# Retention phase: the order of score masks, convolution norm and gates on three engines

## The chip, the core and the metric

The kernel runs on one core of a Trainium2 chip. The metric is the device time of one execution in microseconds. The core's engines run side by side, each through its own instruction queue in order: TensorE (PE, matrix products into PSUM), VectorE (DVE), ScalarE (ACT), GpSimd (POOL) and SyncE (SP, which here only issues DMAs). They are coordinated by semaphores that the program writes out by hand.

## The reference, cut to what is touched

One encoder layer in fp32: 2048 tokens, width 1024. The part around the change is the mixer: four retention heads of width 128, computed in 16 chunks of 128 tokens, in both directions, and a depthwise convolution with 31 taps on 512 channels, each with its own norm and gate.

```python
# retention, one head (k, v per chunk n; both scan directions are summed)
scores = einsum('nqd,nkd->nqk', q, k) * decay          # the mask
state  = chunk_decay * state + kv_n                    # the scans
y      = scores @ v + (q * xi) @ state
y      = (y - mean(y)) * rsqrt(var(y) + EPS) * gn_w + gn_b
y_ret  = silu(proj_g) * y
# convolution group, 512 channels
u      = proj_a * sigmoid(proj_b)
c      = depthwise_conv31(u) + conv_b
c      = layernorm(c) * ln_w + ln_b
y_conv = silu(c)
x      = x + concat([y_ret, y_conv]) @ w_out
```

Cross attention and a squared-ReLU MLP follow; the change doesn't touch them.

## The kernel before

The program has three phases with a barrier between them. Phase one projects the input and runs the convolution's taps; its results go to DRAM (`proj_d`, `conv_d`). Phase two, about 745 to 1025 us, is the retention phase. Phase three has the output projection, the cross attention and the MLP, which take the larger part of the time on TensorE.

In the retention phase each engine goes through heads h = 0 to 3, with the middle heads in a loop (Fori). The convolution's result is normalised beside it: chunk h of 512 tokens, all 512 channels, belongs to head h. It sits in the single buffer `cv` (128 x 4 x 512). The chain of a head is:

- TensorE, `core(h)`: products of keys and values for both scans (L833, L841), scores into banks 0 to 3 (L849), then y into banks 4 to 7 (L860 to L862), in four groups, each after its wait for the masked scores (`s_ev`), then the mean of y (L867). `key_tokens(h+1)` and `value_tokens(h+1)` transpose (L811, L821). `norms(h)` waits for the chunk of the convolution (`c_in`, L870) and for the centred y (`cen`, L871), and then computes the mean of the convolution (L873) and the variances (L877, L880). `spread(h)` (L885) follows.
- VectorE: `scans(h)` (L1604, L1612), `masked_scores(h)` (L1619), `next_rotation(h)` (four rotations of k and q for head h+1, L1583 to L1595; q_rot waits for GpSimd's swapped_q), `norm(h)` (centring L1626, centring of the convolution L1629, reciprocal, scaling L1635). `conv_norm(h-1)` is a reciprocal (L1640) and four products (L1643) on the chunk of the head before.
- ScalarE: `gates(h)` computes the sigmoids of the gate (L1253) and evacuates y in four pieces as TensorE finishes them (L1257); `conv_gates(h-1)` computes sigmoid and affine of the convolution (L1282, L1286), then `key_evac`, `value_evac`, `spreads(h)` (squares, roots), `weighted_values`, `affine(h)`. `spreads(h)` waits until conv_silu(h-1) is done, since it reuses `w1` and `cv_w`.
- GpSimd: `decayed_q` (L580), `gated` (L595), `swapped_k` (L569), `swapped_q` (L573), `silu` of the gate (L587) and `conv_silu` (L600), four products on `cv`.
- SP: the loads, in a fixed order per head. `conv_silu(h)` is followed by the store of `cv` (L437), the wait for that store, and the load of the next chunk into the same buffer (L380, called at L440):

```python
sp.wait_ge(c_out, CT * (h + 1))
sp.dma_start(conv_chunk(y_d[HEADS:HEADS + CT], h), cv[:, :, :]).then_inc(c_st, 16)
if h + 1 < HEADS:
    sp.wait_ge(c_st, 16 * (h + 1))
    load_conv(h + 1)
```

Loads of later heads' operands are issued by SP behind this.

Of the kernel before, what the change touches and what calls it, by code (L numbers as in the profile page):

```python
# [20 lines left out]
def build(nc, x, mem, positions, mix_norm_w, w_in, ret_decay_f, ret_decay_b, ret_gn_w, ret_gn_b,  # L21
# [18 lines left out]
    HEADS = ret_decay_f.shape[1]  # L40
# [48 lines left out]
    with es:  # L89
# [141 lines left out]
        def wait_alone(eng, which, value):  # L231


            eng.wait_ge(which, value)
            eng.sem_inc(passed, 1)
# [266 lines left out]
        def _(pool):  # L502
# [63 lines left out]
            def swapped_k(h):  # L566

                pool.wait_ge(l_ks, 32 * h + 32)
                pool.tensor_tensor(ksb[:, :], ksb[:, :], sin_t[:, :], ALU.mult).then_inc(p_ks, 1)  # L569

            def swapped_q(h):
                pool.wait_ge(l_qs, 32 * h + 32)
                pool.tensor_tensor(qsb[:, :], qsb[:, :], sin_t[:, :], ALU.mult).then_inc(p_qs, 1)  # L573

            def decayed_q(h):
                pool.wait_ge(q_rot, h + 1)
                if not isinstance(h, int) or h:
                    pool.wait_ge(y_mm, 4 * h)
                for dst, xi in ((q_f, xi_f), (q_b, xi_b)):
                    pool.tensor_tensor(dst[:, :].rearrange("p (c q) -> p c q", q=P),  # L580
                                       q_rot_b[:, :].rearrange("p (c q) -> p c q", q=P),
                                       xi[:, bass.ds(h, 1), :].to_broadcast([P, CH, P]), ALU.mult).then_inc(p_qf, 1)

            def silu(h):
                for i in range(4):
                    pool.wait_ge(sgd, 4 * h + i + 1)
                    pool.tensor_tensor(sg[:, i, :], gb[:, i * NC:(i + 1) * NC], sg[:, i, :], ALU.mult).then_inc(gate, 1)  # L587

            def gated(h):
                for i in range(4):  # L590
                    pool.wait_ge(gate, 4 * h + i + 1)
                    pool.wait_ge(y_aff, 4 * h + i + 1)

                    dst = y_stage[:, HEADS - 1, i, :] if isinstance(h, int) and h == HEADS - 1 and i < NH else y_b[:, i, :]
                    pool.tensor_tensor(dst, y_b[:, i, :], sg[:, i, :], ALU.mult).then_inc(y_out, 1)  # L595

            def conv_silu(h):
                for c in range(CT):
                    pool.wait_ge(c_sig, CT * h + c + 1)
                    pool.tensor_tensor(cv[:, c, :], cv[:, c, :], (w1 if c < 2 else cv_w)[:, c % 2, :], ALU.mult).then_inc(c_out, 1)  # L600
# [25 lines left out]
            with pool.Fori(0, HEADS - 2) as h:  # L626
                decayed_q(h + 1)
                gated(h)
                swapped_k(h + 2)
                conv_silu(h)  # L630
                swapped_q(h + 2)
                silu(h + 1)
            decayed_q(HEADS - 1)
            gated(HEADS - 2)
            conv_silu(HEADS - 2)
            silu(HEADS - 1)
            gated(HEADS - 1)
            conv_silu(HEADS - 1)
            leave_phase(pool)
# [423 lines left out]
        def _(act):  # L1063
# [158 lines left out]
            def key_evac(h):  # L1222
                act.wait_ge(kvb_mm, 4 * h)
                for i in range(4):
                    act.wait_ge(kt_mm, 4 * h + i + 1)
                    act.activation(k_tok[:, 4 * i:4 * i + 4, :].rearrange("p c d -> p (c d)"), ps[:, 4 + i, :], ACT.Copy).then_inc(kt_ev, 1)

            def value_evac(h):
                act.wait_ge(y_mm, 4 * h)
                for i in range(4):  # L1230
                    act.wait_ge(vt_mm, 4 * h + i + 1)
                    act.activation(v_tok[:, 4 * i:4 * i + 4, :].rearrange("p c d -> p (c d)"), ps[:, 4 + i, :], ACT.Copy).then_inc(vt_ev, 1)
# [9 lines left out]
            def affine(h):  # L1242

                for i in range(4):
                    wait_alone(act, y_mul, 1 + 4 * h + i + 1)
                    act.activation(y_b[:, i, :], y_b[:, i, :], ACT.Identity, bias=vec[:, bass.ds(V_GNB + h, 1)],
                                   scale=vec[:, bass.ds(V_GNW + h, 1)]).then_inc(y_aff, 1)

            def gates(h):
                act.wait_ge(l_g, 16 * h + 16)  # L1250
                act.wait_ge(y_out, 4 * h)
                for i in range(4):
                    act.activation(sg[:, i, :], gb[:, i * NC:(i + 1) * NC], ACT.Sigmoid).then_inc(sgd, 1)  # L1253
                act.wait_ge(y_st, 16 * h)
                for i in range(4):
                    act.wait_ge(y_mm, 4 * h + i + 1)
                    act.activation(y_b[:, i, :], ps[:, 4 + i, :], ACT.Copy).then_inc(y_ev, 1)  # L1257
# [20 lines left out]
            def conv_gates(h):  # L1278
                for c in range(CT):
                    w, b = vec[:, V_LNW + c:V_LNW + c + 1], vec[:, V_LNB + c:V_LNB + c + 1]  # L1280
                    act.wait_ge(c_mul, CT * h + c + 1)
                    act.activation((w1 if c < 2 else cv_w)[:, c % 2, :], cv[:, c, :], ACT.Sigmoid, bias=b, scale=w).then_inc(c_gat, 1)  # L1282
                for c in range(CT):
                    w, b = vec[:, V_LNW + c:V_LNW + c + 1], vec[:, V_LNB + c:V_LNB + c + 1]
                    act.wait_ge(c_gat, CT * h + c + 1)
                    act.activation(cv[:, c, :], cv[:, c, :], ACT.Identity, bias=b, scale=w).then_inc(c_sig, 1)  # L1286
# [15 lines left out]
            weighted_values(1)  # L1302
            affine(0)
            with act.Fori(1, HEADS - 1) as h:
                conv_gates(h - 1)
                gates(h)
                key_evac(h + 1)
                value_evac(h + 1)
                spreads(h)
                weighted_values(h + 1)  # L1310
                affine(h)
            conv_gates(HEADS - 2)
            gates(HEADS - 1)
            spreads(HEADS - 1)
            affine(HEADS - 1)

# [110 lines left out]
        def _(dve):  # L1427
# [169 lines left out]
            def scans(h):  # L1597

                dve.wait_ge(y_mm, 4 * h)
                for c in range(CH - 1):  # L1600
                    if c % 4 == 0:
                        dve.wait_ge(kvf_mm, 4 * h + c // 4 + 1)
                    dve.wait_ge(f_scan, 15 * h + c)
                    dve.scalar_tensor_tensor(out=st_f[:, c + 1, :], in0=st_f[:, c, :], scalar=gch[:, 0, bass.ds(h, 1)],  # L1604
                                             in1=ps[:, c // 4, (c % 4) * P:(c % 4 + 1) * P],
                                             op0=ALU.mult, op1=ALU.add).then_inc(f_scan, 1)
                for m in range(CH - 1):
                    c = CH - 1 - m
                    if m % 4 == 0:
                        dve.wait_ge(kvb_mm, 4 * h + m // 4 + 1)  # L1610
                    dve.wait_ge(b_scan, 15 * h + m)
                    dve.scalar_tensor_tensor(out=st_b[:, c - 1, :], in0=st_b[:, c, :], scalar=gch[:, 1, bass.ds(h, 1)],  # L1612
                                             in1=ps[:, 4 + c // 4, (c % 4) * P:(c % 4 + 1) * P],
                                             op0=ALU.mult, op1=ALU.add).then_inc(b_scan, 1)

            def masked_scores(h):
                for i in range(4):
                    dve.wait_ge(s_mm, 4 * h + i + 1)
                    dve.tensor_tensor(sT[:, 4 * i:4 * i + 4, :], ps[:, i, :].rearrange("p (c q) -> p c q", c=4),  # L1619
                                      dmask[:, h, :].unsqueeze(1).to_broadcast([P, 4, P]), ALU.mult).then_inc(s_ev, 1)  # L1620
# [16 lines left out]
            def conv_norm(h):  # L1637

                dve.wait_ge(c_std, 1 + h + 1)
                dve.reciprocal(cv_r[:, :], cv_r[:, :]).then_inc(c_rc, 1)  # L1640
                dve.wait_ge(c_rc, h + 1)
                for c in range(CT):
                    dve.tensor_tensor(cv[:, c, :], cv[:, c, :], cv_r[:, :], ALU.mult).then_inc(c_mul, 1)  # L1643
# [26 lines left out]
            norm(0)  # L1670
            with dve.Fori(1, HEADS - 1) as h:
                scans(h)
                conv_norm(h - 1)
                masked_scores(h)
                next_rotation(h)
                norm(h)
            scans(HEADS - 1)
            conv_norm(HEADS - 2)
            masked_scores(HEADS - 1)
            norm(HEADS - 1)  # L1680
            split_low(0, Y_ORDER[:KT - 1])
            conv_norm(HEADS - 1)
# [171 lines left out]
```

## Time and profile before

| | us |
|---|---|
| median of the runs (3) | 3071.07 |
| lowest, highest | 3069.8, 3072.49 |
| profiled execution, its own time | 3074.24 |
| its span, first to last instruction | 3072.2 |
| TensorE busy | 2841.1 (92%) |
| VectorE busy | 1431.3 (47%) |
| GpSimd busy | 940.0 (31%) |
| ScalarE busy | 566.5 (18%) |

Busy shares are means over phases that have different limits. The chain of the page, followed back from the last instruction, is 75% TensorE. Times in a timeline count from the start of the span; a row of several merged instructions (x4) gives the start of the first and the time to the end of the last; what stands in brackets is the idle time before it and what ended it. The granted clock of TensorE is 1.00 at 2.4 GHz and 0.50 at 1.2 GHz.

### The profile page before, as it was taken

To read this page: it belongs to the slowest core of one execution; us is meant where nothing else is said; L and a number is where in the kernel's file an instruction comes from. 1 tells how busy PE (TensorE), PEld (TensorE's weight loads), DVE (VectorE), ACT (ScalarE), POOL (GpSimd) and SP (SyncE) were. 2 spreads that over 40 slices of the span, in tenths; PEclk is the share of its full clock that TensorE was granted. 3 is DMA by queue.
4 is the path that set the end of the run, shared out by engine and by line. 5 is a ranking of instruction groups with operands and counts; after the bars stand their busy time and mean duration, and the time that the engine had idled before them with its cause. 6 is when DMAs were issued, how large, how long until landed. Compare 5 with 4: busy or idle time off the path is not lost.

```text
span 3072.2 us, 37360 instructions
## 1 busy us (share of the span) xinstructions
PE 2841.1 (92%) x13890; PEld 2372.5 (77%) x13890; DVE 1431.3 (47%) x1543; ACT 566.5 (18%) x979; POOL 940.0 (31%) x477
## 2 busy tenths in 40 slices
PE   5899999996686799999999999989999999999997
PEld 4778787876564589888888888868988888888886
DVE  4583939395775443452332414464335324142344
ACT  5211111113345332210000101133221001010012
POOL 4343423333674210033333333321002333333331
PEclk9999999998898899999999999999999999999998
DMA  4133233336542322211111111333221111111111
GB/s 152 51 110 115 100 117 105 116 113 203 162 146 107 96 82 93 80 48 48 48 48 48 48 48 48 102 110 103 83 83 48 48 48 48 48 48 48 48 48 61
DMA packets 289743, 253.83 MB, mean 83 GB/s; under 512 B 8016, under 2 KB 253960, under 8 KB 283400
## 3 DMA queue, kind: packets, MB, share of 16 engines
q1 hardware_dynamic: 265744, 199.26, 20.9%
q10 hardware_dynamic: 23928, 53.58, 4.6%
q8 instruction: 50, 0.82, 0.1%
q14 instruction: 21, 0.17, 0.0%
HBM read 196.71 MB, written 56.10 MB: 82 GB/s over the span
## 4 chain that ended last, share of the span: by engine, by line
PE 75%; DVE 14%; issue 3%; DMA 2%; ACT 2%; POOL 2%; DVEq 0%; ACTq 0%; SPq 0%; POOLq 0%
PE ps L675 22%; PE ps L670 22%; PE ps L671 21%; DVE acc L1516 7%; PE ps L969 2%; PE ps L971 2%; PE ps L970 2%; DVE zfin L1808 1%; POOL cv L600 1%; DVE alo L1649 1%; PE ps L873 1%; DMA wqk_d<-pst 1%; DVE st_b L1612 1%; DVE alo L1782 0%; PE ps L980 0%
## 5 line engine op out<-in xcount | busy, mean ns | idle before, releaser
L521 POOL TENSOR_SCALAR whi<-wraw 128x1024 fp32r<-128x1024 f32 x192 | 228.1, 1188 | 1869.2 <-PE ps L675 1176.1
L670 PE MATMUL ps<-ahi,whi 128*128 128x512 f32 x1408 | 557.4, 396 | 32.3 <-DVE alo L1649 20.4
L671 PE MATMUL ps<-alo,whi 128*128 128x512 f32 x1408 | 551.5, 392 | 0.0
L523 POOL TENSOR_TENSOR wlo<-wraw,whi 128x1024 fp32r<-128x1024 f32 x192 | 531.7, 2770 | 16.0
L670 PE MATMUL ps<-bhi,whi 128*128 128x512 f32 x1024 | 399.4, 390 | 2.3 <-DVE blo L1703 2.3
L671 PE MATMUL ps<-blo,whi 128*128 128x512 f32 x1024 | 398.4, 389 | 0.0
L1516 DVE SCALAR_TENSOR_TENSOR acc<-upad,taps,acc 128x2048 f32<-128x2048 f32 x120 | 346.7, 2889 | 15.7 <-DVE acc L1513 0.6
L675 PE MATMUL ps<-ahi,wlo 128*128 128x512 f32 x1408 | 349.8, 391 | 0.0
L670 PEld LDWEIGHTS ps<-ahi,whi 128*128 128x128 f32 x1408 | 266.3, 189 | 97.0 <-DVE alo L1649 19.3
L1794 DVE TENSOR_TENSOR res<-ps,res 128x512 f32 x128 | 88.6, 692 | 519.7 <-PE ps L675 519.7
L670 PE MATMUL ps<-xhi,whi 128*128 128x512 f32 x768 | 301.7, 393 | 13.4 <-ACT st L1139 7.5
L671 PEld LDWEIGHTS ps<-alo,whi 128*128 128x128 f32 x1408 | 266.5, 189 | 54.5 <-issue 0.5
L675 PEld LDWEIGHTS ps<-ahi,wlo 128*128 128x128 f32 x1408 | 265.4, 189 | 55.8
L671 PE MATMUL ps<-xlo,whi 128*128 128x512 f32 x768 | 300.3, 391 | 0.0
L1389 ACT ACTIVATE ahi<-z 128x512 f32 x128 | 80.9, 632 | 1141.1 <-DVE z L1779 1141.1
L675 PE MATMUL ps<-bhi,wlo 128*128 128x512 f32 x1024 | 252.9, 389 | 0.0
L670 PEld LDWEIGHTS ps<-bhi,whi 128*128 128x128 f32 x1024 | 192.2, 188 | 43.4 <-DVE blo L1703 3.1
L671 PEld LDWEIGHTS ps<-blo,whi 128*128 128x128 f32 x1024 | 192.2, 188 | 40.2 <-issue 0.5
L675 PEld LDWEIGHTS ps<-bhi,wlo 128*128 128x128 f32 x1024 | 192.2, 188 | 40.0
L1782 DVE TENSOR_TENSOR alo<-z,ahi 128x512 f32 x128 | 161.4, 1261 | 120.3 <-ACT ahi L1389 120.3
L675 PE MATMUL ps<-xhi,wlo 128*128 128x512 f32 x768 | 189.7, 389 | 0.0
L1777 DVE TENSOR_TENSOR z<-ps,rstd 128x512 f32<-128x512 f32 x128 | 88.5, 691 | 216.2 <-PE ps L675 215.0
(250 smaller groups left out, 3698.2 us busy)
## 6 DMA issues: line engine op xcount, KB each, us to landing
wraw<-in_w_ff SPq DMA_DIRECT2D x128, 512.0 KB, 3.7
proj_d<-st ACTq DMA_DIRECT2D x64, 256.0 KB, 2.5
wraw<-in_w_in SPq DMA_DIRECT2D x24, 512.0 KB, 4.7
xt<-in_x SPq DMA_DIRECT2D x16, 512.0 KB, 5.6
wraw<-in_w_xkv SPq DMA_DIRECT2D x16, 512.0 KB, 5.9
vwo_d<-pst ACTq DMA_DIRECT2D x16, 512.0 KB, 3.6
wqk_d<-pst ACTq DMA_DIRECT2D x16, 512.0 KB, 2.8
wraw<-in_w_out SPq DMA_DIRECT2D x16, 512.0 KB, 4.7
```

The source lines that it names most:

```text
L521: pool.tensor_scalar(whi[:, slot, :, :], wraw[:, slot, :, :], 1.0, 0.0, ALU.mult, ALU.add).then_inc(w_hi, 1)
L523: pool.tensor_tensor(wlo[:, slot, :, :], wraw[:, slot, :, :], whi[:, slot, :, :], ALU.subtract).then_inc(w_ready, 1)
L670: nc.tensor.matmul(o, whi[:, slot, k, :], hi(k), start=(k == order[0]), stop=False)
L671: nc.tensor.matmul(o, whi[:, slot, k, :], lo(k), start=False, stop=False)
L675: last = nc.tensor.matmul(o, wlo[:, slot, k, :], hi(k), start=False, stop=(k == order[-1]))
L969: pe.matmul(o, a, high[:, k * M:(k + 1) * M], start=(k == 0), stop=False)
L970: pe.matmul(o, a, low[:, k * M:(k + 1) * M], start=False, stop=False)
L1389: act.activation(ahi[:, 2 * i + s, n, :], z[:, n, :], ACT.Copy).then_inc(hi_done, 1)
L1516: ins = dve.scalar_tensor_tensor(out=acc[:, :], in0=src, scalar=taps[:, bass.ds(CT * t + c, 1)], in1=acc[:, :], op0=ALU.mult, op1=ALU.add)
L1777: dve.tensor_tensor(z[:, n, :], ps[:, 2 * s + n, :], rstd[:, n, :], ALU.mult).then_inc(bank_free, 1)
L1782: dve.tensor_tensor(alo[:, 2 * i + s, n, :], z[:, n, :], ahi[:, 2 * i + s, n, :], ALU.subtract).then_inc(lo_done, 1)
L1794: dve.tensor_tensor(res[:, m, n, :], ps[:, 2 * s + n, :], res[:, m, n, :], ALU.add).then_inc(bank_free, 1)
```

## The change

Three engines get another order of the same calls; nothing is added or removed. On VectorE `masked_scores(h)` comes right behind `scans(h)`, and `conv_norm(h-1)` follows. On ScalarE `gates(h)`, with the evacuations of y, comes before `conv_gates(h-1)`. On GpSimd `silu(h+1)` and `swapped_q(h+2)` come before `conv_silu(h)`. Heads 1 and 2 run in the loops, head 3 in the lines behind them; head 0 keeps its order.

```diff
--- before.py
+++ after.py
@@ -627,13 +627,13 @@
                 decayed_q(h + 1)
                 gated(h)
                 swapped_k(h + 2)
+                silu(h + 1)
+                swapped_q(h + 2)
                 conv_silu(h)
-                swapped_q(h + 2)
-                silu(h + 1)
             decayed_q(HEADS - 1)
             gated(HEADS - 2)
+            silu(HEADS - 1)
             conv_silu(HEADS - 2)
-            silu(HEADS - 1)
             gated(HEADS - 1)
             conv_silu(HEADS - 1)
             leave_phase(pool)
@@ -1302,15 +1302,15 @@
             weighted_values(1)
             affine(0)
             with act.Fori(1, HEADS - 1) as h:
+                gates(h)
                 conv_gates(h - 1)
-                gates(h)
                 key_evac(h + 1)
                 value_evac(h + 1)
                 spreads(h)
                 weighted_values(h + 1)
                 affine(h)
+            gates(HEADS - 1)
             conv_gates(HEADS - 2)
-            gates(HEADS - 1)
             spreads(HEADS - 1)
             affine(HEADS - 1)
 
@@ -1670,13 +1670,13 @@
             norm(0)
             with dve.Fori(1, HEADS - 1) as h:
                 scans(h)
+                masked_scores(h)
                 conv_norm(h - 1)
-                masked_scores(h)
                 next_rotation(h)
                 norm(h)
             scans(HEADS - 1)
+            masked_scores(HEADS - 1)
             conv_norm(HEADS - 2)
-            masked_scores(HEADS - 1)
             norm(HEADS - 1)
             split_low(0, Y_ORDER[:KT - 1])
             conv_norm(HEADS - 1)
```

## Rows read from the trace of the kernel before

**Rows 1.** Stretches: us, busy per engine (instructions), granted clock, DMA share, GB/s

```profile
824.96:883.45 58.49, 43.33 (x266) 32.00 (x265) 41.91 (x57) 28.95 (x43) 40.98 (x16) 0.91 0.41 146
883.45:941.93 58.48, 45.04 (x268) 33.68 (x267) 41.90 (x58) 29.04 (x44) 40.97 (x16) 0.88 0.27 88
```

**Rows 2.** Chain of waits inside head 1: start us, us, what

```profile
844.25 2.12 POOL cv L600 x2
...
848.77 6.59 POOL cv L600 x2
...
855.36 4.49 POOL q_sw L573
...
863.22 2.40 DVE y_b L1626 x4
...
865.76 5.37 PE ps L873 x8
```

**Rows 3.** VectorE's timeline, head 1: start us, us, line, operation [idle before]

```profile
836.42 3.35 DVE L1640 RECIPROCAL cv_r<-cv_r 128x512 f32<-128x512 f32 x1
...
839.81 2.50 DVE L1643 TENSOR_TENSOR cv<-cv,cv_r 128x512 f32<-128x512 f32 x4
...
842.22 2.48 DVE L1619 TENSOR_TENSOR sT<-ps,dmask 128x512 f32<-128x512 f32 x4
...
844.62 3.05 DVE L1583 TENSOR_TENSOR k_in<-k_in,cos_t 128x2048 f32<-128x2048 f32 x1
```

**Rows 4.** TensorE's timeline, first products of y, heads 0 and 1

```profile
780.65 0.46 PE L860 MATMUL ps<-sT,v_tok 128*128 128x128 f32 x2 [1.00 <-DVE sT L1619]
...
843.05 0.77 PE L860 MATMUL ps<-sT,v_tok 128*128 128x128 f32 x2 [8.49 <-DVE sT L1619]
```

**Rows 5.** SP's timeline, head 1: DMA issues

```profile
855.38 0.38 SPq L437 DMA_DIRECT2D y_d<-cv  x1
...
859.40 0.38 SPq L380 DMA_DIRECT2D cv<-conv_d  x1
```

**Rows 6.** DMA issues of head 1: KB each, median us from issue to landing

```profile
cv<-conv_d SPq DMA_DIRECT2D x1, 1024.0 KB, 5.0
```

**Rows 7.** Stretch in which TensorE's granted clock falls (columns as Rows 1)

```profile
839.00:839.50 0.50, 0.00 (x0) 0.00 (x0) 0.50 (x1) 0.00 (x0) 0.00 (x0) 0.63 0.00 0
```

**Rows 8.** ScalarE's timeline: fourth evacuations of heads 0 and 1, conv_gates of head 1

```profile
791.64 0.60 ACT L1257 ACTIVATE y_b<-ps 128x512 f32<-128x512 f32 x1 [2.08 <-PE ps L862]
...
840.53 1.52 ACT L1282 ACTIVATE w<-cv,vec 128x512 f32<-128x512 f32 x2 [11.57 <-DVE cv L1643]
...
855.43 0.60 ACT L1257 ACTIVATE y_b<-ps 128x512 f32<-128x512 f32 x1 [2.08 <-PE ps L862]
```

**Rows 9.** GpSimd's timeline: swapped_k of head 1, conv_silu beside head 3

```profile
830.63 4.52 POOL L569 TENSOR_TENSOR k_sw<-k_sw,sin_t 128x2048 f32<-128x2048 f32 x1
...
961.39 2.52 POOL L600 TENSOR_TENSOR cv<-cv,w 128x512 f32<-128x512 f32 x2 [13.66 <-ACT cv L1286]
...
963.87 2.51 POOL L600 TENSOR_TENSOR cv<-cv,cv_w 128x512 f32<-128x512 f32 x2
```

**Rows 10.** Timelines of GpSimd and VectorE, rotations of head 0

```profile
795.13 4.50 POOL L573 TENSOR_TENSOR q_sw<-q_sw,sin_t 128x2048 f32<-128x2048 f32 x1
...
795.28 6.50 DVE L1588 TENSOR_TENSOR k_rot<-k_in,k_sw 128x2048 f32<-128x2048 f32 x1 [10.24 <-POOL k_sw L569]
...
801.70 2.28 DVE L1592 TENSOR_TENSOR q_in<-q_in,cos_t 128x2048 f32<-128x2048 f32 x1
```

**Rows 11.** Timelines of VectorE and GpSimd at the MLP's norm

```profile
1320.01 6.56 DVE L1712 RECIPROCAL rstd<-rstd 128x512 f32<-128x512 f32 x2 [3.64 <-ACT rstd L1354]
...
1325.75 1.05 POOL L521 TENSOR_SCALAR whi<-wraw 128x1024 fp32r<-128x1024 f32 x1 [10.54 <-PE ps L675]
```

**Rows 12.** TensorE's timeline, first convolution mean of head 3

```profile
977.95 3.67 PE L873 MATMUL ps<-cv,mean_mat 128*128 128x512 f32 x8 [0.87 <-DVE y_b L1626]
```

**Rows 13.** VectorE's timeline, end of head 3's backward scans

```profile
953.58 3.35 DVE L1640 RECIPROCAL cv_r<-cv_r 128x512 f32<-128x512 f32 x1
```

## The prediction

> **What bounds the kernel now.** The page's chain gives TensorE 75% of the span, but that is an average; the change touches only the retention phase, about 745 to 1025 us. So I cut the trace by head first. From the first scan of head 1 to the first scan of head 2 pass 58.49 us, and the next head takes 58.48 us [rows 1]: a periodic loop, in which whatever ends last sets the period. Then I read the chain of waits inside head 1 [rows 2]: GpSimd's conv_silu of the previous chunk (L600) ends at 855.36, then swapped_q (L573), then VectorE's q_rot (L1595), then the centring of y (L1626) until 865.62, then TensorE's first convolution mean (L873) at 865.76. The reader should see that the scores' products are not in this chain: y is late, but it is hidden behind GpSimd's queue. VectorE's timeline [rows 3] shows what the change is after: the backward scans end at 836.42, conv_norm takes until 842.22, and only then are the scores masked; TensorE sits idle 8.49 us for them [rows 4].
>
> There is a second input of L873 that the chain doesn't show, since it comes a little earlier. `cv` is one buffer. The chunk of head h is loaded only when chunk h-1 has been stored, and that store follows conv_silu(h-1) (L436 to L440). SP issues the store at 855.38, the load at 859.40 [rows 5], and the load lands 5.0 us later [rows 6], at 864.4. So L873 waits for the centring until 865.62 and has the chunk 1.2 us before. **That slack of 1.2 us is all there is**, in head 1 and, with the same spacings, in head 2. I call C the time from conv_silu's end to the chunk's landing: 864.4 - 855.36 = 9.05 us.
>
> **The change, part by part, in head 1.** Every instruction is kept; only orders move on three engines.
>
> VectorE. The masks start at 836.42 instead of 842.22, 5.8 us earlier; they need only the scores' products, which are long done. conv_norm follows at 838.82 (the masks take 844.62 - 842.22 = 2.40). Its reciprocal takes 3.39, to 842.21 [rows 3].
>
> TensorE. y starts 0.83 us after the first mask (843.05 against 842.22), so at 837.25. The idle time before it falls from 8.49 to 2.7 us [rows 3, 4]. In the kernel before, the granted clock stayed full until about 839.2 and then fell to half, 1.2 GHz [rows 7]; y would now start before that point. Head 0, whose y starts after 1.00 us idle, shows the undisturbed length: from 780.65 to ScalarE's last evacuation at 791.64, which ends at 792.24: 11.6 us [rows 4, 8]. With it the last evacuation ends at 848.85. If the clock falls all the same, it takes the 13.0 us that head 1 took before (843.05 to 855.43 + 0.60) [rows 4, 8], to 850.2.
>
> ScalarE. conv_gates(0) no longer waits for VectorE but stands behind the fourth evacuation. It used to begin at 840.53, and GpSimd had its first operand at 844.25 [rows 2, 8]: 3.7 us. Now that is 848.85 + 3.7 = 852.6. What queues behind conv_gates on ScalarE is key_evac and value_evac; they get 5.8 us later than the evacuations allow, which the wait for the chunk (below) covers. If that cover went, the key evacuations at about 854.7 would still be earlier than before.
>
> GpSimd. swapped_k(2) ends at 835.15 [rows 9]; silu(1) needs 5.0 uncontended, swapped_q(2) 4.5, so these end at 840.1 and 844.6, where before they stood behind conv_silu. VectorE's q_rot no longer waits for them. conv_silu(0) itself takes 5.0 us where nothing disturbs it (961.39 to 966.38) [rows 9], but it can't start before 852.6. It meets VectorE there. When both work on SBUF operands they take turns by whole instructions: VectorE's k_rot, issued at 795.28, took 6.50 us, since GpSimd's instruction from 795.13 ran until 799.6, and the same shape alone takes 2.28 [rows 10]. The reciprocal doesn't take part: GpSimd's 128x1024 split ran its 1.05 us beside the reciprocals of 1320.01 to 1326.57 [rows 11]. No row shows L1643 (two SBUF operands) beside GpSimd. Its cost lies between 0 and the rest of swapped_q, 844.6 - 842.2 = 2.4 us; I take 2.4, by the nearest row, k_rot, which has the same operation and two SBUF operands. The Trainium skill, "SBUF — State Buffer", section "Who interferes with whom", says that a VectorE instruction with two SBUF inputs and a GpSimd instruction reading SBUF exclude each other for a whole instruction; by that rule it is 2.4 too, and without the rule it could be 0.
>
> So L1643 ends at 847.0, and k_in, k_rot and q_in at 2.2 us each run to 853.6. conv_silu's first piece waits for q_in, runs to 854.85, q_rot then holds GpSimd until 857.05, and three pieces of 1.25 follow: **conv_silu ends at 860.8**, 5.4 us later than before. With the slower y its start falls at 854, behind q_rot (855.8), and it ends at 860.8 too. If L1643 were not blocked, rotations would be over at 851.2 + 2.2 and it would end at 858.5. So 858.5 and 860.8 are the bounds, and the clock of y doesn't matter.
>
> SP. Store and load of the chunk stand behind conv_silu; nothing else is in front of them. C is unchanged at 9.05, as load_g and the rotations' loads are issued behind the chunk's. It lands at 869.85 instead of 864.4. The centring is done at about 857.1 + 2.4 = 859.5. L873 starts at 870.0 instead of 865.76: **+4.2 us**, where the slack took 1.2 of the 5.4. Everything up to the next head's scans hangs on L873. TensorE has then been idle for 12 us instead of 3.44 and starts at half clock; L873 took 5.37 in head 1 with a mixed clock against 3.67 at full [rows 2, 12]. I add 0.5 (bounds 0 and 1.7). Heads 1 and 2: 2 x 4.7 = 9.4.
>
> **Head 3** has no rotations, so before it was bound by y itself: L873 started at 977.95, right behind the centring, and at full clock [rows 12]. Now: masks from 953.58, where the reciprocal stood [rows 13]; y from 954.4, last evacuation over at 966.0; conv_silu from 969.7 to 974.7; chunk at 983.8; L873 at 984.0, 6.0 later. It starts cold, 5.37 instead of 3.67: +1.7. Together 7.7, and with a half-clock y 1.4 to 2.5 more. The rest of the phase (division, splits, last conv_norm, store) follows L873 as before. The seven y_stage loads are issued behind the chunk's load and move with it; they are needed some 20 us after it.
>
> Sum: 9.4 + 7.7 = 17.1 us on a profiled run of 3074.24 us (span 3072.2); the median is 3071.07, so 3088.2. I round to **3088**.
>
> **Rivals.**
> 1. *The chunk comes in time, the gain arrives.* If conv_silu's round trip were hidden, L873 would follow the centring: 859.6 against 865.76, -6.2 in heads 1 and 2, and in head 3 -5.2 to -7.7 with the full clock: about -19, 3052. For it: the idle of 8.49 us is real. It decides from the point at which the chunk lands before the centring is done (859.5). Against: by the rows the chunk lands 10 us after that, and the two DMAs alone are 9. The Trainium skill, "TensorE: Matmul & The Clock Gate", section "Why this matters for your kernels", asks for short idle times between bursts; that would be served at y and violated at L873. Chance 0.06.
> 2. *It cancels.* L873 would have to start within 2 us of where it does, a round trip partly hidden. By L1643 unblocked, heads 1 and 2 give +1.9 each and no clock loss, head 3 +6: 3081. For no change within 0.2% (6.1 us), head 3 would have to be free as well. Chance 0.07.
> 3. *The order has no effect*, since the evacuations' waits let ScalarE reach conv_gates at once: the rows of y say no, as the last evacuation is 11.6 us behind y's start. It is inside rival 2.
> 4. *More slower:* the cold clock takes 1.7 in each head and y of head 3 runs at half clock: 17.1 + 2.4 + 2.5 = 22, 3093; if cut instructions interleave worse (three rotations against three pieces, 2.2 us more per head) 3097. Chance 0.12.
>
> The forecast, a round trip of the conv chunk that ends last and L873 4 to 8 us later per head, has 0.75. Range 3079 to 3097: it reaches to the unblocked L1643 with no loss of clock below, and to the cold clock with worse interleaving above. 0.2% (6 us) is about what a measurement of this kernel can tell from no change. Faster 0.06, same 0.07, slower 0.87.
>
> **What would show it.** In the profile after: masks (L1619) at scans' end, idle of TensorE before y near 2.7 us, y at full clock; conv_gates behind the fourth evacuation; conv_silu ending some 35.8 us after the head's first scan (30.4 before); TensorE idle before L873 of about 12 us, ended by the chunk's DMA and not by L1626; period near 63 us instead of 58.5. Wrong, if L873 still waits for the centring, if C is not 9 us, or if the time moves outside 745 to 1025 us.

## The result, and the profile after

| | before | after |
|---|---|---|
| median, us | 3070.44 (4 runs, 3069.42 to 3072.49) | 3090.01 (4 runs, 3088.84 to 3092.52) |
| profiled execution, us | 3074.24 | 3089.29 |
| its span, us | 3072.2 | 3087.2 |

The changed kernel is slower by 19.6 us, a ratio of 1.0064 with a 95% interval from 1.0048 to 1.008. The forecast was 3088 (3079 to 3097).

First the same cut by head, which answers to [rows 1]. The columns are as there: start and end, length, busy time of TensorE, of its weight loads, of VectorE, ScalarE and GpSimd, then TensorE's granted clock, the share of the DMA engines and what they moved:

```profile
824.84:888.53 63.69, 45.03 (x266) 32.66 (x265) 40.28 (x57) 28.82 (x43) 34.44 (x16) 0.87 0.45 148
888.53:951.03 62.50, 42.83 (x268) 30.79 (x267) 41.38 (x57) 29.00 (x43) 35.93 (x16) 0.89 0.18 68
```

The first scan of head 1 stands at the same place, 0.12 us apart, and then each head is longer: head 1 by 5.20 us, head 2 by 4.02 us. The chain of waits inside head 1 of the changed kernel, against [rows 2]:

```profile
856.89 3.74 POOL cv L600 x3
...
860.65 3.99 DMA y_d<-cv
...
864.65 5.04 DMA cv<-conv_d
...
869.73 6.47 PE ps L873 x8
```

GpSimd's swapped_q and the centring (L1626) are gone from it. Their place is taken by the store of the convolution's chunk and the load of the next one, which follow conv_silu and take 9.03 us. TensorE's timeline shows what it waits for (to be read with [rows 4, 12]):

```profile
837.14 0.46 PE L860 MATMUL ps<-sT,v_tok 128*128 128x128 f32 x2 [2.69 <-DVE sT L1619]
...
869.73 6.47 PE L873 MATMUL ps<-cv,mean_mat 128*128 128x512 f32 x8 [11.10 <-DMA cv<-conv_d]
933.28 5.43 PE L873 MATMUL ps<-cv,mean_mat 128*128 128x512 f32 x8 [12.61 <-DMA cv<-conv_d]
994.36 5.61 PE L873 MATMUL ps<-cv,mean_mat 128*128 128x512 f32 x8 [14.82 <-DMA cv<-conv_d]
```

The change does what it was meant to do: the idle time before y falls from 8.49 to 2.69 us. But a longer one opens before L873, 11 to 15 us, and in each of the three heads it is the chunk's load that ends it. In head 3 L873 had run at full clock (3.67 us); now it starts at half clock and takes 5.61.

The timelines of VectorE, ScalarE and GpSimd in head 1, against [rows 3, 8]:

```profile
836.31 2.48 DVE L1619 TENSOR_TENSOR sT<-ps,dmask 128x512 f32<-128x512 f32 x4
838.70 3.34 DVE L1640 RECIPROCAL cv_r<-cv_r 128x512 f32<-128x512 f32 x1
842.08 4.65 DVE L1643 TENSOR_TENSOR cv<-cv,cv_r 128x512 f32<-128x512 f32 x4
846.66 2.28 DVE L1583 TENSOR_TENSOR k_in<-k_in,cos_t 128x2048 f32<-128x2048 f32 x1
...
855.71 2.48 DVE L1626 TENSOR_TENSOR y_b<-y_b,ps 128x512 f32<-128x512 f32 x4
...
849.76 0.60 ACT L1257 ACTIVATE y_b<-ps 128x512 f32<-128x512 f32 x1 [2.08 <-PE ps L862]
850.26 1.51 ACT L1282 ACTIVATE w<-cv,vec 128x512 f32<-128x512 f32 x2
...
839.85 4.53 POOL L573 TENSOR_TENSOR q_sw<-q_sw,sin_t 128x2048 f32<-128x2048 f32 x1
853.96 4.21 POOL L600 TENSOR_TENSOR cv<-cv,w 128x512 f32<-128x512 f32 x2 [9.58 <-ACT cv L1286]
```

The centring L1626 is over at 858.19, 11.5 us before L873 starts. It was the last input before and now has a wide margin. ScalarE begins conv_gates (L1282) right behind the fourth evacuation, and GpSimd sits idle 9.58 us for it before conv_silu (L600). VectorE's products L1643 begin while swapped_q runs until 844.38 and take 4.65 us instead of 2.50.

The barrier at the phase's end gives the sum of the retention phase. VectorE's first instruction behind it, before and after:

```profile
1025.03 0.06 DVE L1688 MEMSET junk<- 128x1 f32 x1 [6.55 <-SPq L239]
```

```profile
1042.72 0.06 DVE L1688 MEMSET junk<- 128x1 f32 x1 [5.90 <-SPq L239]
```

That is 17.69 us: 5.20 for head 1, 4.02 for head 2, 8.59 for head 3 and the phase's end, less the 0.12 of the start. The spans of these two executions differ by 15.0 us and the medians by 19.6. The profiled execution of before was 3.8 us above its median (3074.24 against 3070.44), that of after 0.7 below (3089.29 against 3090.01). Behind the barrier the change touches nothing. From there to the end the thirteen profiles of this case (the two here and those below) take from 2044.2 to 2048.3 us; the 2.7 us by which these two differ there lie inside that spread.

### The profile page after: what moved, and what is told of

Same layout as the page of the kernel before. It is cut to its first block, busy times and chain, and to the rows that moved or that the text cites. A ratio compares the mean times of both kernels' runs of the same rounds, so it can differ in the third digit from the quotient of the medians.

```text
span 3087.2 us, 37360 instructions
## 1 busy us (share of the span) xinstructions
PE 2845.6 (92%) x13890; PEld 2374.1 (77%) x13890; DVE 1426.9 (46%) x1543; ACT 566.6 (18%) x979; POOL 928.8 (30%) x477
## 4 chain that ended last, share of the span: by engine, by line
PE 76%; DVE 14%; DMA 3%; issue 3%; ACT 2%; POOL 2%; DVEq 0%; ACTq 0%; SPq 0%; POOLq 0%
PE ps L675 22%; PE ps L670 22%; PE ps L671 21%; DVE acc L1516 7%; PE ps L969 2%; PE ps L971 2%; PE ps L970 2%; DVE zfin L1808 1%; POOL cv L600 1%; PE ps L873 1%; DVE alo L1649 1%; DVE xlo L1448 1%; DMA wqk_d<-pst 1%; DMA y_d<-cv 1%; PE ps L931 1%
```

## The experiments

**Theory 1**, that of the forecast: what ends last in a head is the way of the convolution's chunk through the single buffer: evacuations of y, conv_gates, conv_silu, store, load, L873. **Theory 2**, the rival: the cost comes from engines in each other's way on the compute side (VectorE and GpSimd taking turns at L1643, conv_norm 2.4 us later, the evacuations ahead of conv_gates), and the DMAs are hidden or incidental.

The table gives what each kernel showed. The columns h1, h2 and h3 are the start of L873 behind the head's first scan (L1604), in us. The column "phase" is the time from the first scan of head 1 to the barrier, in us; it leaves out the parts that no edit touches. Both come from one profiled execution each. The kernel before ran again beside each group: its medians were 3072.62 (the four kernels below the change), 3073.48 (the next four) and 3071.99 (the last three). So kernels of different groups are compared by their ratios or by the phase, not by their medians.

| kernel | median | ratio to before (95%) | h1 | h2 | h3 | phase |
|---|---|---|---|---|---|---|
| before | 3070.44 | | 40.80 | 40.79 | 36.02 | 200.07 |
| the change | 3090.01 | 1.0064 (1.0048 to 1.008) | 44.89 | 44.75 | 43.33 | 217.88 |
| VectorE's part alone | 3077.39 | 1.0013 (1.0003 to 1.0023) | 41.24 | 41.23 | 35.98 | 203.26 |
| change, ScalarE put back | 3106.46 | 1.0107 (1.009 to 1.0124) | 51.71 | 51.75 | 43.32 | 232.08 |
| change, GpSimd put back | 3088.77 | 1.0052 (1.0035 to 1.0068) | 42.80 | 42.80 | 41.62 | 213.26 |
| change, chunks not loaded | 3077.27 | 1.0013 (1.0004 to 1.0023) | 39.89 | 40.03 | 38.35 | 204.18 |
| change, tiles | 3089.43 | 1.0056 (1.004 to 1.0073) | 43.87 | 46.01 | 42.68 | 216.25 |
| before, tiles | 3070.58 | 0.9989 (0.998 to 0.9999) | 40.77 | 40.78 | 36.20 | 197.79 |
| before, tiles, swapped_q first | 3060.84 | 0.9965 (0.9954 to 0.9977) | 37.48 | 37.94 | 35.94 | 188.03 |
| ScalarE's part alone | 3113.01 | 1.0133 (1.0116 to 1.015) | 51.26 | 51.01 | 49.60 | 236.13 |
| change, tiles, later loads held | 3082.79 | 1.0037 (1.0024 to 1.0049) | 41.64 | 43.47 | 40.33 | 207.87 |
| before, swapped_q first | 3067.31 | 0.9984 (0.9974 to 0.9993) | 39.48 | 39.56 | 35.33 | 192.49 |
| tiles, swapped_q first, head 3 masks first | 3062.24 | 0.9966 (0.9955 to 0.9978) | 38.12 | 38.38 | 33.25 | 187.92 |

Of the eight combinations of the three engines' moves six were run: GpSimd's part alone, and GpSimd's together with ScalarE's, were not.

### VectorE's part alone

```diff
                 scans(h)
+                masked_scores(h)
                 conv_norm(h - 1)
-                masked_scores(h)
                 next_rotation(h)
```

and the same for head 3; ScalarE and GpSimd as before.

> Only VectorE's order of the change; ScalarE and GpSimd as before. Theory 1 (the conv chunk's store and load behind conv_silu end last): ScalarE takes conv_gates as soon as VectorE's product is there, one masks' length later than before (2.4 us), so conv_silu ends about 31.2 us after the head's first scan instead of 30.4; the chunk lands 40.2 after it, about where L873 started before (40.8). Heads 1 and 2 within 0.5 us of before, head 3 within 0 to 2 (L873 from a colder clock). Total 3070 to 3073. Theory 2 (what costs is VectorE and GpSimd taking turns at L1643, and VectorE's later conv_norm): the delay of conv_norm by 2.4 us passes on, +2.4 per head, 3078.

L873 is 0.4 us later in heads 1 and 2 and at its place in head 3:

```profile
866.24 5.78 PE L873 MATMUL ps<-cv,mean_mat 128*128 128x512 f32 x8 [7.72 <-DVE y_b L1626]
...
979.01 5.74 PE L873 MATMUL ps<-cv,mean_mat 128*128 128x512 f32 x8 [5.76 <-DMA cv<-conv_d]
```

The median lies 4.8 us above before (ratio 1.0013). That is more than theory 1's 0 to 3, and taken alone it would suit theory 2 (3078). The places of L873 decide: the delay of conv_norm by 2.4 us per head, which theory 2 wanted, does not pass on. In the profile the phase is 3.2 us longer, of which the second row shows 2.07: in head 3 L873 starts at half clock and takes 5.74 us instead of 3.67. Masking first buys nothing by itself: y is ready sooner, but the centring still waits for swapped_q behind conv_silu, and in head 3 the chunk takes over as the last input.

### The change with ScalarE's order put back

```diff
-                gates(h)
                 conv_gates(h - 1)
+                gates(h)
                 key_evac(h + 1)
```

Head 3 is put back in the same way.

> The change with ScalarE's order put back: conv_gates ahead of the gates, while GpSimd keeps silu and swapped_q ahead of conv_silu. Theory 1: conv_silu now stands behind silu, whose sigmoids come only after conv_gates; silu about 14 us later than in the change, swapped_q behind it, conv_silu ends about 40 us after the head's first scan instead of 35.8, L873 some 4 to 5 us later in heads 1 and 2, the same in head 3: 3097 to 3101, slower than the change. Theory 2 (ScalarE's evacuations ahead of conv_gates are what delays conv_silu, and nothing else): putting them back recovers most of the loss, 3075 or less.

It is slower still, by 13 us against the change (ratio 1.0107 against 1.0064). Putting back ScalarE's part recovers nothing, since GpSimd's new order depends on it. GpSimd's timeline:

```profile
849.84 6.95 POOL L587 TENSOR_TENSOR sg<-g_in,sg 128x512 f32<-128x512 f32 x4 [14.14 <-ACT sg L1253]
856.75 4.52 POOL L573 TENSOR_TENSOR q_sw<-q_sw,sin_t 128x2048 f32<-128x2048 f32 x1
861.24 4.53 POOL L600 TENSOR_TENSOR cv<-cv,w 128x512 f32<-128x512 f32 x2
```

GpSimd's silu waits 14.14 us for sigmoids that stand behind conv_gates, and swapped_q and conv_silu wait in the queue behind it. The sign and the place were as theory 1 had them, and the size was not: L873 moved 6.8 and 7.0 us in heads 1 and 2 where 4 to 5 had been expected, and the median lies above the 3097 to 3101. About 2 us of it come from q_rot, which took its turn between two pieces of conv_silu (4.53 instead of 2.5).

### The change with GpSimd's order put back

```diff
                 swapped_k(h + 2)
-                silu(h + 1)
-                swapped_q(h + 2)
                 conv_silu(h)
+                swapped_q(h + 2)
+                silu(h + 1)
```

> The change with GpSimd's order put back: conv_silu, swapped_q, silu. Theory 1: swapped_q is no longer beside L1643, so L1643 takes 2.5 us again; conv_silu starts behind ScalarE's fourth evacuation all the same and ends some 34 us after the first scan (35.8 in the change), L873 then 1 to 2 us earlier in heads 1 and 2; head 3 unchanged: 3086 to 3089. q_rot and the centring come later, near 43 us, close to the chunk's landing. Theory 2 (turns at L1643 make the loss): 3080 or less.

```profile
845.41 2.50 DVE L1643 TENSOR_TENSOR cv<-cv,cv_r 128x512 f32<-128x512 f32 x4
...
870.97 6.64 PE L873 MATMUL ps<-cv,mean_mat 128*128 128x512 f32 x8 [10.64 <-DVE y_b L1626]
```

In head 3 conv_silu goes ahead of silu again too. L1643 takes 2.50 us again instead of 4.65, so the turns at L1643 were real. conv_silu ends 32.5 us after the first scan instead of 35.8, 3.3 us earlier, since L1643 is over sooner and conv_silu too runs undisturbed. L873 gains only 2.1 and 2.0 us of it in heads 1 and 2, because the centring, now behind swapped_q again, becomes the last input there, at 42.8. Head 3, expected unchanged, gains 1.7 us: no turns were taken there in either kernel, but y ran at full clock (11.6 us to the fourth evacuation, 13.2 in the change). Together that is 4.6 us in the phase and 0.12% in the ratio (1.0052 against 1.0064, and the intervals overlap). Most of the loss stays, so the turns are a part of it and not what makes it.

### The change without the loads of chunks 1 to 3

```diff
-                pe.wait_ge(c_in, 16 * h + 16)
+                pe.wait_ge(c_in, 16)
+                pe.wait_ge(c_st, 1 + 16 * h)
...
                 if h + 1 < HEADS:
-                    sp.wait_ge(c_st, 16 * (h + 1))
-                    load_conv(h + 1)
+                    sp.wait_ge(c_st, 1 + 16 * (h + 1))
...
```

(The semaphore `c_st` is raised by one at the start, so that head 0 doesn't wait for a store.)

> The change, but chunks 1 to 3 of the convolution are not loaded: L873 waits for the store of the chunk before only and works on what stands in the buffer (the norm and gate run on old values; the store stays). Theory 1: the 5.0 us of the load drop out of the path in each of heads 1 to 3: L873 at about 40 us after the first scan, released by the store's DMA; 15 us less in all, 3074 to 3076. Theory 2 (GpSimd and VectorE in each other's way, or the clock, make the loss): the load is hidden and the time stays within 2 us of the change, 3088 to 3091.

```profile
864.43 5.93 PE L873 MATMUL ps<-cv,mean_mat 128*128 128x512 f32 x8 [6.10 <-DMA y_d<-cv]
922.72 5.80 PE L873 MATMUL ps<-cv,mean_mat 128*128 128x512 f32 x8 [6.25 <-DMA y_d<-cv]
```

L873 moves up by 5.0, 4.7 and 5.0 us, and its releaser is now the store. The ratio falls from 1.0064 to 1.0013, about 15 us, and the phase is 13.7 us shorter. No compute instruction was moved. That shows theory 1 directly: the load lies on the path in all three heads, at nearly its full length of 5.0 us. Theory 2, by which the DMAs are hidden, falls here. What stays true of it is that the delays on the compute side reach L873 through conv_silu's end.

### The change with the chunk moved in four tiles

```diff
-                sp.wait_ge(c_out, CT * (h + 1))
-                sp.dma_start(conv_chunk(y_d[HEADS:HEADS + CT], h), cv[:, :, :]).then_inc(c_st, 16)
-                if h + 1 < HEADS:
-                    sp.wait_ge(c_st, 16 * (h + 1))
-                    load_conv(h + 1)
+                for c in range(CT):
+                    sp.wait_ge(c_out, CT * h + c + 1)
+                    sp.dma_start(y_d[HEADS + c, :, h * NC:(h + 1) * NC], cv[:, c, :]).then_inc(c_tile[c], 16)
+                if h + 1 < HEADS:
+                    for c in range(CT):
+                        sp.wait_ge(c_tile[c], c_base[c] + 16 * (h + 1))
+                        sp.dma_start(cv[:, c, :], conv_d[c, :, (h + 1) * NC:(h + 2) * NC]).then_inc(c_in, 16)
...
```

> The change, with the chunk's store and load cut into its four channel tiles, each with its own semaphore: a tile is stored as soon as its product is there and loaded again as soon as its store has landed. Theory 1: what counts is the last tile's store and load, 256 KB each, about 2.5 and 2.8 us, instead of 9.05: L873 some 3.7 us earlier in heads 1 to 3, and about 2.5 us less at the phase's end, where the last chunk's store is waited for: 13 to 14 us less than the change, 3076 to 3079. Theory 2 (engines in each other's way, or the clock, make the loss): only the phase's end is shorter, 3088 to 3090.

This is a miss: the kernel takes 3089.43 us, ratio 1.0056. Taken alone, the time is what theory 2 had said (3088 to 3090). L873 gains 1.0 us in head 1 and 0.7 in head 3 and loses 1.3 in head 2. SP's timeline, and what the view of `cv` gives for its DMAs in the stretch:

```profile
859.90 2.32 SPq L445 DMA_DIRECT2D cv<-conv_d  x4
862.26 0.43 SPq L379 DMA_DIRECT2D g_in<-proj_d  x1
862.74 0.43 SPq L366 DMA_DIRECT2D k_in<-proj_d  x1
```

```profile
DMA to landing us min/median/max: 2.3/4.0/5.9
```

In heads 1 and 3 the last tile's store took 2.3 us, about as expected; in head 2 it took 3.6. The last tile's load, 256 KB, took 5.9, 6.4 and 6.0 us in the three heads, longer than the whole 1024 KB load of the change (5.04). So the part behind conv_silu is hardly shorter than before. Other loads were issued right behind the last tile's, and they may be what slows it. That is a hypothesis at this point; the kernel with the later loads held back, below, tests it.

### The kernel before with tiles

The same edit on the kernel before.

> The kernel before with the same tiled store and load, all orders as before. Theory 1: heads 1 and 2 are bound there by GpSimd's queue and the centring, not by the chunk, so L873 doesn't move; only the store at the phase's end is shorter by 2.5 us: 3068 to 3070. If the chunk already bound the kernel before, it would be 3058 to 3062.

```profile
864.89 5.37 PE L879 MATMUL ps<-cv,mean_mat 128*128 128x512 f32 x8 [3.26 <-DVE y_b L1632]
```

(L879 and L1632 are L873 and L1626 of the kernel before.) L873 stays within 0.2 us in all heads, ended by the centring: before the change the chunk was not what ended last. The ratio is 0.9989, about 3 us; in the profile the phase is 2.3 us shorter, and all of that lies behind head 3's scans, where the last chunk is stored in smaller pieces.

### Tiles, and swapped_q ahead of conv_silu

On top of that, one move of the change's, on GpSimd:

```diff
                 swapped_k(h + 2)
+                swapped_q(h + 2)
                 conv_silu(h)
-                swapped_q(h + 2)
                 silu(h + 1)
```

> The kernel before with the tiled store and load, and on GpSimd swapped_q ahead of conv_silu, which is one of the change's moves; silu stays last, VectorE and ScalarE as before. Theory 1: both inputs of L873 move up. The centring no longer waits for conv_silu and ends about 35 us after the head's first scan (40.7 before), bound by y; the chunk lands at about 36. L873 is 4.5 us earlier in heads 1 and 2, none in head 3; with the shorter last store 11.5 us less than before, 3059 to 3062. If only one of the two had been binding, the gain would be 2.5 to 4 us.

The median is 3060.84, 12.6 us less than that of the kernel before beside it; the ratio of 0.9965 makes it 10.7, and the phase is 12.0 us shorter. It is faster than both kernels of the case. The chain in head 1:

```profile
857.72 1.75 PE ps L817 x16
859.47 1.75 PE ps L827 x16
861.22 3.44 PE ps L879 x8
```

(L817, L827 and L879 are L811, L821 and L873 of the kernel before.) TensorE goes from the transposes into the convolution's mean without an idle time and at full clock (3.44 against 5.37). So neither the chunk nor the centring is what L873 waits for any more, but TensorE's own work in front of it. L873 starts 3.3 and 2.9 us earlier, less than the 4.5 expected, and the clock adds about 1.8 per head.

### ScalarE's part alone

```diff
+                gates(h)
                 conv_gates(h - 1)
-                gates(h)
                 key_evac(h + 1)
```

and the same for head 3.

> Only ScalarE's order of the change (gates and the evacuations of y ahead of conv_gates), VectorE and GpSimd as before: y is as late as before, and conv_gates now waits for it. Theory 1: conv_silu ends about 39.8 us after the head's first scan, L873 at 49 instead of 40.8, and in head 3 at 50.3 instead of 36: 8.7 us more in each of heads 1 and 2, 16 more in head 3: 3104 to 3108, worse than the whole change, since the masks' earlier place takes 5.8 us off that very path. Theory 2 (the masks ahead of conv_norm make the loss): 3073, as before.

```profile
863.09 2.50 POOL L600 TENSOR_TENSOR cv<-cv,w 128x512 f32<-128x512 f32 x2 [25.71 <-ACT cv L1286]
...
878.42 5.22 PE L873 MATMUL ps<-cv,mean_mat 128*128 128x512 f32 x8 [10.65 <-DVE y_b L1626]
```

This is the slowest of all: 3113.01, ratio 1.0133, above the 3104 to 3108 expected. Alone, ScalarE's move costs most, since GpSimd waits 25.71 us for conv_gates. It is not the only one that can harm: VectorE's and GpSimd's moves without it (the change with ScalarE's order put back) gave 1.0107. In heads 1 and 2 L873 came 2 us later than expected, and behind the centring, since swapped_q too stands behind conv_silu here; head 3 came at 49.60 against 50.3 expected. The masks' move (VectorE's part) takes 5.8 us off the same path, which is why the whole change costs less than this part of it.

### The change with tiles, and later loads held back

On top of the change with tiles, one wait is added:

```diff
                         sp.dma_start(cv[:, c, :], conv_d[c, :, (h + 1) * NC:(h + 2) * NC]).then_inc(c_in, 16)
+                    sp.wait_ge(c_in, 64 * (h + 2))
```

> The change with the tiled store and load, and SP holds back the loads of later heads (and of y_stage) until the chunk's four tiles have landed. In the run with tiles alone the last tile's load took 5.9 us although its store took 2.4, with g_in and k_in issued 0.4 us behind it. If these followers share the DMA engines with it, the load now takes 2.5 to 3 us, L873 comes about 41 us after the head's first scan instead of 43.9, and the kernel takes 9 us less than with tiles alone, 3079 to 3082. If the small load is slow for itself, nothing changes, 3088 to 3090.

```profile
861.32 2.34 DMA y_d<-cv
...
863.67 3.67 DMA cv<-conv_d
...
867.38 5.63 PE ps L880 x8
```

The last tile now loads in 3.67 us instead of 5.9, with nothing changed but what is issued behind it. In heads 1 and 3 store and load behind conv_silu take 6.0 us together, in head 2 7.4 (9.03 in the change). L873 is 2.2 to 2.5 us earlier than with tiles alone in every head. So the loads issued behind a small one do slow it here, and the miss of the kernel with tiles is not for theory 2. The load is still 1 us slower than the 2.5 to 3 expected. Of the 9 us the phase shows 8.4 and the medians 6.6; 3082.79 lies just above the 3079 to 3082 expected.

### The kernel before with swapped_q first, chunk whole

```diff
                 swapped_k(h + 2)
+                swapped_q(h + 2)
                 conv_silu(h)
-                swapped_q(h + 2)
```

> The kernel before with swapped_q ahead of conv_silu on GpSimd and nothing else; store and load of the chunk whole. Theory 1: the centring is 5 us earlier, so the chunk becomes the last input of L873 in heads 1 and 2, at 30.4 + 9.05 = 39.5 us after the first scan instead of 40.8: 1.2 us per head, and up to 1.7 more where TensorE's clock holds: 3067 to 3071, released by the chunk's DMA in the profile. If the chunk's round trip were not what ends last, L873 would follow the centring at 35: 3060.

```profile
864.36 3.70 PE L873 MATMUL ps<-cv,mean_mat 128*128 128x512 f32 x8 [0.74 <-DMA cv<-conv_d]
```

L873 starts 39.48 and 39.56 us behind the first scan, where 39.5 had been worked out from conv_silu's end and C (the time from that end to the chunk's landing), and it is released by the DMA. One move of one call makes the centring early, and L873 then starts 1.3 and 1.2 us earlier than before, with the chunk as its last input: that is the slack that the rows of before showed. The ratio is 0.9984. conv_silu ends 30.4 us after the first scan as before, although swapped_q now stands in front of it:

```profile
835.02 4.51 POOL L573 TENSOR_TENSOR q_sw<-q_sw,sin_t 128x2048 f32<-128x2048 f32 x1
844.16 4.56 POOL L600 TENSOR_TENSOR cv<-cv,w 128x512 f32<-128x512 f32 x2 [4.63 <-ACT cv L1286]
```

swapped_q runs in idle time that GpSimd spends waiting for ScalarE anyway.

### Head 3 with its masks first, on the fastest kernel

To the kernel with tiles and swapped_q first this move is added, and SP holds the `y_stage` loads back until chunk 3 has landed:

```diff
             scans(HEADS - 1)
+            masked_scores(HEADS - 1)
             conv_norm(HEADS - 2)
-            masked_scores(HEADS - 1)
...
```

> The kernel with tiled store and load and swapped_q first, and in head 3 alone VectorE masks the scores ahead of conv_norm; SP holds the y_stage loads back until chunk 3 has landed. Theory 1: in head 3 y is 5 us earlier and the chunk lands about 32 us after the first scan, L873 at 33 instead of 36, but at half clock at first, +1.7: 0 to 3 us less than without it, 3056 to 3061.

```profile
968.91 5.40 PE L881 MATMUL ps<-cv,mean_mat 128*128 128x512 f32 x8 [3.03 <-DMA cv<-conv_d]
```

(L881 is L873 of the kernel before.) In head 3 L873 comes at 33.25, as expected, instead of 35.94, but takes 5.40 us instead of 3.67: 1.7 of the 2.7 us gained go back to the clock. The remaining 1 us is less than this measurement can tell from nothing (3062.24, ratio 0.9966 against 0.9965), and the 3056 to 3061 expected was missed.

## Why the prediction was right, step by step

- **The slack of 1.2 us and the round trip C.** C was worked out as 9.05; after, it is 869.69 - 860.63 = 9.06. The kernel with only swapped_q moved confirms the slack: L873 stops at 39.5.
- **conv_silu's end**: 860.8 forecast, 35.8 us behind the first scan; measured 860.63 and 35.79. For L1643 beside GpSimd no row of before stood, and 2.4 us were taken from k_rot's row. It took 2.15 more in head 1 (4.65 instead of 2.50) and 2.33 in head 2 (4.83).
- **L873 in heads 1 and 2**: +4.2 forecast, +4.09 and +3.96 measured. For the clock 0.5 per head was taken, between bounds of 0 and 1.7; 1.10 and 0.06 were measured (6.47 and 5.43 against 5.37). Together 9.4 against 9.22; that the sum for the clock came so near is luck.
- **Head 3**: 7.7 forecast, 8.59 measured. L873 came 7.31 later, not 6.0. The term that was mis-sized is y's length: it was taken at full clock, 11.6 us, and took 13.2 (963.51 to 976.73). The forecast had named this case, "with a half-clock y 1.4 to 2.5 more", but had left it out of its sum. The clock's loss on L873 was 1.94 for 1.7; 0.65 came back in the last store.
- **y's clock in general** was the step that failed: after an idle time of 2.7 us y was expected at full clock. It held in head 2 and not in heads 1 and 3 (below). In head 1 it didn't matter, as had been said, because conv_silu's first piece then waits for q_rot and its end stays where it was: conv_silu ended 35.8 us behind the first scan in head 1 and 35.6 in head 2.
- **Sum**: 17.1 forecast against 17.69 at the barrier and 19.6 in the medians. The rivals in which the chunk comes in time or the effects cancel did not occur; of the one named "more slower", y at half clock in head 3 came in part.

## What to carry to other kernels

Before moving work ahead of other work on several engines, list for the next join every input with its landing time, not only the one that the chain names: here the second one landed only 1.2 us ahead of the last, and the change delayed it by 5.4. A single buffer that is stored and reloaded within a loop is a path of its own, and the work that ends it (here conv_gates and conv_silu) belongs early in its engines' queues, even if its result isn't needed soon. In front of it belongs only what fits into the time in which the engine would wait anyway, as swapped_q did. Idle time of the busiest engine that a change removes is only gained if no other wait stands behind it: TensorE lost 5.8 us of idle time before y and got 8 to 14 more before L873.

## What the runs showed of the hardware beyond what was expected

TensorE's clock can fall after the work has resumed. From 837.14 on TensorE was busy with y, after an idle time of only 2.69 us, and the granted clock fell all the same. That happened in heads 1 and 3 and not in head 2. The stretches of head 1 of the changed kernel, columns as Rows 1:

```profile
837.00:837.50 0.50, 0.36 (x3) 0.39 (x4) 0.50 (x1) 0.00 (x0) 0.50 (x2) 1.00 0.00 0
837.50:838.00 0.50, 0.50 (x6) 0.50 (x6) 0.50 (x2) 0.00 (x0) 0.50 (x1) 0.81 0.00 0
838.00:838.50 0.50, 0.50 (x4) 0.50 (x4) 0.50 (x2) 0.00 (x0) 0.50 (x1) 0.50 0.00 0
...
841.50:842.00 0.50, 0.50 (x7) 0.50 (x6) 0.50 (x1) 0.28 (x1) 0.50 (x1) 1.00 0.00 0
```

It cost 1.6 us: from y's start to the end of the fourth evacuation pass 13.22 us in head 1 and 11.59 in head 2. The profiles of this case have 22 starts of y behind an idle time of 2.3 to 2.7 us. In 14 of them the clock fell to half within some 2 us of the resumed work, in 8 it stayed full; with the chunks not loaded it fell in all three heads, with GpSimd put back in none. What decides between the two isn't shown. The Trainium skill, "TensorE: Matmul & The Clock Gate", section "Why this matters for your kernels", asks for short idle times between bursts of matmuls; by these rows 2.7 us is not short enough in every head.

A small load is not quick when other loads are issued right behind it. 256 KB took 5.9 us with a load of 1024 KB issued 0.4 us behind it and seven more following one after another, and 3.67 us with them held back. The whole load of 1024 KB took 5.04 us with the same followers and 5.0 in the kernel before, where they come 7 us later. Why the small load suffers and the large one doesn't isn't shown.

The reciprocal ran its 3.34 us undisturbed beside GpSimd's silu and swapped_q, as the rows of the norm [rows 11] had suggested, while L1643 waited for its turn.
